# Splitting the first weight units of three stages ahead of the layer norm in a 256-token, four-layer kernel

## What is computed

```python
for layer in range(DEPTH):                      # DEPTH = 2
    if layer < N_A_LAYERS:                      # layer 0: recurrent mixer
        mix = hgrn2_mixer(h, hgrn_w_in[layer], ...)
    else:                                       # layer 1: sliding-window attention
        mix = swa_sink_mixer(h, k_shared, v_shared, swa_w_q[j], ...)
    h = layer_norm_2(ALPHA_2 * h + mix, ln_mix_g[layer], ln_mix_b[layer])
    ff = conv_ffn(h, ffn_w_in[layer], ffn_conv_w[layer], ffn_conv_b[layer], ffn_w_out[layer])
    h = layer_norm_2(ALPHA_2 * h + ff, ln_ffn_g[layer], ln_ffn_b[layer])
    if layer == N_A_LAYERS - 1:
        k_flat, v_flat = jnp.split(h @ shared_w_kv, 2, axis=-1)
...
def conv_ffn(h, w_in, conv_w, conv_b, w_out):
    u = h @ w_in                                # 1024 -> 2 x 2816
    u = causal depthwise conv of width 3 (u) + conv_b
    a, b = jnp.split(u, 2, axis=-1)
    return (jax.nn.silu(a) * b) @ w_out
```

## Time and profile before

| | us |
|---|---|
| median of 3 runs | 1653.82 (1653.15 to 1654.51) |
| the profiled execution | 1651.92 |
| its span | 1650.1 |
| PE busy | 1457.9 (88%) |
| DVE busy | 607.3 (37%) |
| ACT busy | 455.8 (28%) |
| POOL busy | 120.4 (7%) |

### The profile page before, as it was taken

How to read it: one execution, slowest core, us unless ns; L and a number is a source line. 1 busy time by engine, 2 the same in 40 slices (tenths; PEclk the granted TensorE clock), 3 DMA queues, 4 the chain that set the end, 5 groups by cost and what they waited for, 6 DMA issues and landing times.

```text
span 1650.1 us, 20157 instructions
## 1 busy us (share of the span) xinstructions
PE 1457.9 (88%) x7744; PEld 949.6 (58%) x7744; DVE 607.3 (37%) x1231; ACT 455.8 (28%) x851; POOL 120.4 (7%) x135
## 2 busy tenths in 40 slices
PE   6978699999699787999986989759999797899997
PEld 4854543343267545334333988449984384599943
DVE  0253311111212622101114489467850424487602
ACT  1252211111122511111112423136640234276500
POOL 1011000000000300000002054030000003000000
PEclk9989799999899897999997999879999898899999
DMA  9430399999926024999998525735654440355530
GB/s 326 163 102 1 142 388 393 397 394 392 366 84 224 32 98 174 392 397 393 393 397 263 168 95 105 155 127 181 209 186 153 141 152 1 119 162 194 214 127 25
DMA packets 185375, 347.45 MB, mean 211 GB/s; under 512 B 8209, under 2 KB 84263, under 8 KB 185317
## 3 DMA queue, kind: packets, MB, share of 16 engines
q1 hardware_dynamic: 179920, 330.19, 56.1%
q0 software_dynamic: 4528, 15.84, 4.0%
q10 hardware_dynamic: 868, 0.63, 0.1%
HBM read 342.44 MB, written 4.19 MB: 210 GB/s over the span
## 4 chain that ended last, share of the span: by engine, by line
PE 76%; DVE 8%; SPq 7%; ACT 3%; DMA 3%; issue 2%; DVEq 0%; POOL 0%; ACTq 0%
PE bank L1446 16%; PE bank L1645 9%; PE bank L1880 9%; SPq L577 7%; PE bank L1762 7%; PE bank L1763 7%; PE bank L1764 7%; PE bank L1655 5%; PE bank L1666 3%; PE bank L1706 3%; DMA slot<-in_w_down 2%; PE bank L1797 2%; ACT arena L748 1%; ACT arena L711 1%; DVE res L1025 1%
## 5 line engine op out<-in xcount | busy, mean ns | idle before, releaser
L1762 PE MATMUL bank<-x_high,w_high 128*128 128x256 f32 x912 | 262.8, 288 | 17.9 <-DVE w_low L1365 14.3
L1763 PE MATMUL bank<-x_low,w_high 128*128 128x256 f32 x912 | 261.9, 287 | 0.0
L1764 PE MATMUL bank<-x_high,w_low 128*128 128x256 f32 x912 | 261.7, 287 | 0.0
L1645 PE MATMUL bank<-slot,arena 128*64 128x512 f32 x1024 | 223.7, 594 | 1.6 <-DMA slot<-in_w_up 1.5
L711 ACT ACTIVATE arena<-bank 128x512 f32<-128x512 f32 (+7 forms) x196 | 99.4, 533 | 370.4 <-PE bank L1655 121.8
L1762 PEld LDWEIGHTS bank<-x_high,w_high 128*128 128x128 f32 x912 | 179.2, 197 | 20.4 <-DVE w_low L1365 14.9
L1763 PEld LDWEIGHTS bank<-x_low,w_high 128*128 128x128 f32 x912 | 179.2, 197 | 0.0
L1764 PEld LDWEIGHTS bank<-x_high,w_low 128*128 128x128 f32 x912 | 179.1, 196 | 0.0
L711 ACT ACTIVATE w_high<-slot 128x1024 fp32r<-128x1024 f32 x130 | 130.0, 1050 | 120.1 <-PE bank L1764 91.0
L1645 PEld LDWEIGHTS bank<-slot,arena 128*64 128x64 f32 x1024 | 72.5, 137 | 149.7 <-issue 149.7
L1880 PE MATMUL bank<-slot,arena 128*128 128x512 f32 x352 | 151.4, 592 | 0.0
(11 more groups left out here) (257 smaller groups left out, 1661.1 us busy)
## 6 DMA issues: line engine op xcount, KB each, us to landing
slot<-in_w_gate SPq DMA_DIRECT2D x64, 1024.0 KB, 14.0
slot<-in_w_up SPq DMA_DIRECT2D x64, 1024.0 KB, 14.2
slot<-in_w_down SPq DMA_DIRECT2D x64, 1024.0 KB, 13.9
slot<-in_ffn_w_in SPq DMA_DIRECT2D x44, 1024.0 KB, 7.4
slot<-in_ffn_w_out SPq DMA_DIRECT2D x22, 1024.0 KB, 5.0
slot<-in_hgrn_w_in SPq DMA_DIRECT2D x16, 1024.0 KB, 6.0
slot<-in_w_in SPq DMA_DIRECT2D x10, 1024.0 KB, 11.3
slot<-in_w_o SPq DMA_DIRECT2D x8, 1024.0 KB, 7.1
```

The costliest lines, as they stand in the source:

```text
L1645: last = mm(banks_gu["gu".index(m)][rows, :], B["xe"][:, 4 * half + c, rows], ws[e][:, c, :], start=(half == 0 and c == 0), stop=(half == ...
L1762: mm(dst, high[:, k, :], x_high[:, k, :], start=(k == 0), stop=False)
L1763: mm(dst, high[:, k, :], x_low[:, k, :], start=False, stop=False)
L1764: last = mm(dst, low[:, k, :], x_high[:, k, :], start=False, stop=(k == KD - 1))
```

## The change

`split` becomes `split_ffn`, a function outside `feed_forward`, on ScalarE and on VectorE. The splits of the first step's two units are called ahead of the norm in both engines' lists, in layers 2 and 3; so are the splits of `kv0` and `sq0`, ahead of norm 5. Nothing is added and nothing is left out; TensorE, GpSimd and SyncE have the lists of before.

```diff
@@ scalar
+            def split_ffn(l, j, i, c):
+                for ab, n in enumerate("ab"):
+                    raw = slot(loaded(act, (l, f"F{n}{j}"), i), KD, 256)
+                    copy(w_high[c][:, ab, :, :], raw[:, :, P * c:P * (c + 1)]).then_inc(sem("high_ready"), 1)
             def feed_forward(l):
...
-                for c in range(2):
-                    split(0, 0, c)
                 with act.Fori(0, STEPS // 2 - 1) as i:
...
             recurrent()
+            for c in range(2):
+                split_ffn(2, 0, 0, c)
             norm_std(4)
             transposed_split(2, "y")
             feed_forward(2)
-            norm_std(5)
-            transposed_split(2, "z", whole=True)
             names = ["kv0"] + [f"sq{i}" for i in range(4)]
             for n in range(2):
                 split_slot(3, names[n], KV_UNIT + n)
+            norm_std(5)
+            transposed_split(2, "z", whole=True)
...
             softmax_heads(3, SWQ, G["prob"], G["probT"], G["mixT"], sink=True)
+            for c in range(2):
+                split_ffn(3, 0, 0, c)
             norm_std(6)
@@ vector
+            def split_ffn(l, j, i, c):
+                before_ = 2 * (FFN_UNIT[l] + c + (2 * STEPS - 2 if i is None else 2 * j)) + (0 if i is None else 8 * i)
+                for ab, n in enumerate("ab"):
+                    raw = slot(W[(l, f"F{n}{j}")], KD, 256)
+                    dve.wait_ge(sem("high_ready"), before_ + (ab + 1))
+                    V.tensor_tensor(w_low[c][:, ab, :, :], raw[:, :, P * c:P * (c + 1)], w_high[c][:, ab, :, :].bitcast(F32), ALU.subtract)\
+                        .then_inc(sem("split"), 1)
...
-                for c in range(2):
-                    split(0, 0, c)
                 with dve.Fori(0, STEPS // 2 - 1) as i:
...
             recurrent()
+            for c in range(2):
+                split_ffn(2, 0, 0, c)
             norm(4, 2, "y", True)
             feed_forward(2)
+            names = ["kv0"] + [f"sq{i}" for i in range(4)]
+            for n in range(2):
+                low_slot(3, names[n], KV_UNIT + n)
             norm(5, 2, "z", True)
...
-            for n, name in enumerate(["kv0"] + [f"sq{i}" for i in range(4)]):
-                low_slot(3, name, KV_UNIT + n)
+            for n in range(2, 5):
+                low_slot(3, names[n], KV_UNIT + n)
...
+            for c in range(2):
+                split_ffn(3, 0, 0, c)
             norm(6, 3, "y", True)
             feed_forward(3)
```

More of the change, by code:

```diff
@@ L938, in feed_forward @@
                 drained(copy(F["cw"], b[:, 0:4 * CH].rearrange("p (k n) -> p k n", k=4)), (l, "cw"))
[L940 to L944, removed]
                 def step(j, i, following):
@@ L951, in step @@
                         if following:
-                            split(*following, c)
+                            split_ffn(l, *following, c)
                         if c == 0:
@@ L1357, in feed_forward @@
                 cw = F["cw"].rearrange("p k (a n) -> p k a n", a=2)
[L1359 to L1366, removed]
                 def step(j, i, following):
```

## The result

| | before | after |
|---|---|---|
| median | 1653.92 us (4 runs, 1653.15 to 1654.51) | 1634.96 us (4 runs, 1634.31 to 1637.2) |
| profiled execution | 1651.92 | 1634.31 |
| its span | 1650.1 | 1632.5 |

The ratio is 0.9888, with a 95% interval of 0.9871 to 0.9905: 19.0 us less, between 15.7 and 21.3. The forecast was 1639.2 with a range of 1636.0 to 1643.0. The same kernel was measured twice more later, on other occasions, with 1637.59 and 1635.95 us (gains of 15.4 and 16.7).

A forecast was written before the change was run, and what follows sets the result against it. The prediction took TensorE to bound the kernel, with holes where it waited on w_low subtracts. Savings of 11.2 + 1.2 + 2.2 = 14.6 us, taken from a three-run median of 1653.82, gave 1639.2 us, range 1636.0 to 1643.0.

The forecast's parts named there:

- Bound and carry-through: TensorE, 76% of the last-ending chain, bounds the kernel; time won in holes at the feed-forwards' starts reaches the end.
- The cause of the long hole: First feed-forward: a 10.21 us VectorE w_low subtract, median 1.22, was held some 9 us by GpSimd's bias addition.
- rival 2: First feed-forward loop: GpSimd's addition holds the tap copies and the first subtracts behind them; costs 0.3 us, 1639.5; chance 0.08.
- I take 0.44: First feed-forward: TensorE needs 0.44 us from the cw transposes' end to the first matmul, bounds 0.05 and 1.04.
- the terms 11.2 and 2.2: Microseconds won by TensorE's earlier first matmul: 11.2 in the first feed-forward, 2.2 in the last.
- the key projection's 1.2: Key projection: splitting kv0 and sq0 early starts TensorE at 1316.34, not 1317.52; 1.2 us won (0.6 to 1.6).
- I take nothing: TensorE's 1.2 GHz stretches after resuming at the three places change the total by zero, with 2 us either way.
- Cover: First feed-forward: moved splits fit idle ScalarE and VectorE time; norm operations begin 1.3 us late, at no cost.
- at most one for one past 1058.1: First feed-forward: each microsecond the b weight load lands past 1058.1 may delay the norm by one; expected landing 1054.0.
- Rival 1: Feed-forward loop entries: TensorE's issue gap, up to 2.3 us, is exposed; both loops lose 3.7 us, 1642.9; chance 0.10.
- Rival 3: Norm 4 waits behind a late b load; slower than before if landing past 1072.7; 1659.8 at 58 us load; chance 0.02.
- Rival 4: No effect: TensorE waits at the same places on something else read as ready; 1653.8 us; chance 0.02.

The follow-up runs named there:

- e_before_add16: Kernel before the change, with GpSimd's bias addition cut into 16 back-to-back instructions of one head each; 1652.59 us against 1652.49.
- r_after: The changed kernel unchanged, measured a second time against the kernel before on the same chip; 1637.59 us against 1652.97.
- r_after2: The changed kernel unchanged, measured a third time against the kernel before; 1635.95 us against 1652.66.
- e_after_late_b: Changed kernel with the first feed-forward's Fb0 weight load held back until the projection's third bank is full; 1645.85 us against 1635.95 for the changed kernel.
- e_after_late_b1: Changed kernel with the first feed-forward's Fb0 weight load held back until the projection's second bank is full; 1640.17 us against 1635.95 for the changed kernel.

## Why the prediction missed its range

- **Bound and carry-through: right.** Each hole closed in TensorE's queue, and what was won there reached the end; the first feed-forward's products run as densely as before.
- **The cause of the long hole: right.** GpSimd's addition holds a VectorE operation that reads only SBUF: shown by taking it away (9.0 us) and by its passing to the tap copy (10.31 us), which the prediction named. That such a hold is one GpSimd instruction long, as in rival 2, is too narrow: in `e_before_add16` it ran through 16.
- **"I take 0.44": too much.** The loop's entry and the issue behind the transposes cost nothing; TensorE's first matmul follows at once, and its record even overlaps them. The lower bound, 0.05 us, was right. The 0.44 us had been measured behind a wait, and is in the hole once already, ahead of the transposes. This step of the prediction failed; it undersized the terms 11.2 and 2.2 as 11.75 and 2.7; the key projection's 1.2, where the matmul itself follows the wait, measured 1.27. Sum of the holes: 15.7, not 14.6.
- **"I take nothing" for the clock: off by 1.1 us in the profiled pair.** The low stretch of the first feed-forward was 3.18 us and not 5.18. It doesn't belong to the change alone: counted from the matmul's record, the stretch was 3.6 us here, 4.2 in `r_after` and 3.4 in `r_after2`, and with the splits behind the norm 5.3 in the kernel before and 3.2 in `e_before_add16`. The 2 us either way covered it.
- **The step that took the time out of the range: the scatter of the runs, put at nothing.** With 15.7 for the holes and 1.1 for the clock the prediction's sum gives 1637.0, inside its range. But the sum was put on the median of three runs that lay 1.4 us apart. In 21 executions beside each other the kernel before took 1651.1 to 1654.7, the changed one between 1634.3 and 1638.5 in its three comparisons. The range held the bounds of the change's own costs and nothing for the two medians; 1.5 us more on each side would have held all three measurements. By the profiled pair, the miss of 4.2 us is 1.1 (issue), 1.1 (clock), 0.75 (stages ahead) and 1.4 (medians against profiled executions), less the 0.1 by which the kernel before then measured above 1653.82. So the sizes that were wrong explain 2.2 of it and the scatter 2.0; the size of that scatter is shown, its cause is not.
- **Cover: right, and larger than said.** The subtracts made the norm's first operations 0.5 us late (4.83 us of idle time behind them, not 5.37) and cost nothing. Beyond that the rule "at most one for one past 1058.1" gave up to 18 and 12 us for the two late loads, which landed at 1075.9 and 1070.4; 9.9 and 4.2 were measured, because the first row tile has idle time of its own.
- **Rivals.** Rival 1 fell: no issue gap at the loops. Rival 2 happened as a mechanism, at a price of zero. Rival 3 is a real mechanism, but a load that comes 23 us later (`e_after_late_b`, 1075.9 and not 1052.7) still leaves the kernel 6.8 us faster than before. Rival 4 fell.
- SyncE's four loads, issued from 1077.2 to 1082.5, took 10.2 us in the median where two took 6.4; nothing waited for them, as said.

What stays open: why the first comparison gave 19.0 us. Its interval holds the 16.1 of the holes, and the scatter seen is of that size; no run ties the rest to anything in the change.

## What to carry to other kernels

Work that needs only a load (here splitting a weight in two) should stand in each engine's list ahead of work that needs the last product, wherever the engine is idle; but it then makes everything behind it wait for that load, so compare the landing with the first time at which the engine is wanted. When one instruction of a line is many times longer than its median, look at what GpSimd does in that moment before you move or shorten anything: the hold moved on here to the next VectorE operation that reads only SBUF, and it matters only where that one is waited for. For a gain of 1%, put the scatter of the two medians into the range as a term of its own.

## What the runs showed of the hardware

- A GpSimd addition on SBUF held a VectorE subtract with two SBUF inputs (10.2 us for 1.22) and a VectorE single-input copy of 128 x 8 elements (10.3 us for 0.17). It did not hold subtracts with one input in PSUM (0.69 us).
- Unexpected: cutting that addition into 16 instructions doesn't let VectorE in between (12.3 us hold, pieces of 0.98 us started every 0.95 us), but a semaphore wait between the pieces does (longest subtract 2.03 us).
- After resuming at the 1.2 GHz level TensorE got the 2.4 GHz level 2.9 us (`e_after_late_b1`) to 5.3 us (kernel before) later at the same place of the program (first feed-forward); in three executions of the changed kernel it was 3.4, 3.6 and 4.2 us.
